# Expert stage of a hybrid encoder: 96 token slots per expert sweep instead of 128

## The reference

```
def moe_swiglu(x, w_router, w_gate, w_up, w_down):
    """Top-2-of-8 SwiGLU experts, softmax over the selected logits (Mixtral)."""
    b, s, d = x.shape
    xt = x.reshape(b * s, d)
    logits = (xt @ w_router).astype(jnp.float32)
    top_val, top_idx = lax.top_k(logits, TOP_K)
    top_w = jax.nn.softmax(top_val, axis=-1)
    gates = jnp.sum(jax.nn.one_hot(top_idx, N_EXPERTS, dtype=jnp.float32) * top_w[..., None], axis=1)
    gates = gates.astype(x.dtype)
    y = jnp.zeros_like(xt)
    for e in range(N_EXPERTS):
        y = y + gates[:, e:e + 1] * swiglu(xt, w_gate[e], w_up[e], w_down[e])
    return y.reshape(b, s, d)
```

## Time and profile before

| | us |
|---|---|
| median of three runs | 1445.77 |
| lowest and highest run | 1441.11, 1446.24 |
| span of the profiled execution | 1439.2 |
| PE busy | 1415.5 |
| DVE busy | 1133.4 |
| ACT busy | 967.7 |
| POOL busy | 127.0 |

### The profile page before, as it was taken

The page is one execution under the profiler, slowest core; times in us unless marked ns, Lnnn a source line. Parts: engine busy times, 40 slices in busy tenths (PEclk is TensorE's granted clock), DMA queues, the critical chain, the costliest instruction groups (busy, mean ns, idle before and its releaser), DMA issues.

```text
span 1439.2 us, 20918 instructions
## 1 busy us (share of the span) xinstructions
PE 1415.5 (98%) x7689; PEld 1215.3 (84%) x7689; DVE 1133.4 (79%) x896; ACT 967.7 (67%) x885; POOL 127.0 (9%) x101
## 2 busy tenths in 40 slices
PE   9989999999999999999999999999999999999996
PEld 8888999999997888888888888888888888888885
DVE  4764555556665988898898898889899898888886
ACT  6574443446574677777777777777777777777774
POOL 4430000000000410010020001002002001000100
PEclk9999999999999999999999999999999999999999
DMA  9306855555432899999999999999999999999992
GB/s 337 131 1 205 243 187 175 185 194 176 147 115 91 307 386 372 368 383 393 380 365 396 381 355 394 387 346 387 395 384 373 394 368 360 394 375 367 397 396 100
DMA packets 205562, 434.91 MB, mean 302 GB/s; under 512 B 8160, under 2 KB 53344, under 8 KB 205520
## 3 DMA queue, kind: packets, MB, share of 16 engines
q1 hardware_dynamic: 198176, 418.01, 79.7%
q0 software_dynamic: 3904, 14.42, 3.3%
q10 hardware_dynamic: 3440, 1.91, 0.7%
HBM read 426.98 MB, written 7.34 MB: 302 GB/s over the span
## 4 chain that ended last, share of the span: by engine, by line
PE 95%; DVE 2%; ACT 1%; DMA 0%; issue 0%; DVEq 0%; SPq 0%; ACTq 0%
PE banks L1501 29%; PE banks L1503 29%; PE banks L1502 29%; PE banks L1734 2%; PE banks L1955 2%; PE banks L1722 1%; DVE w_lo L928 1%; PE banks L1919 0%; PE banks L1659 0%; DMA xres<-in_x 0%; PE banks L1677 0%; PE banks L1709 0%; PE banks L1593 0%; PE banks L1901 0%; PE banks L1527 0%
## 5 line engine op out<-in xcount | busy, mean ns | idle before, releaser
L928 DVE TENSOR_TENSOR w_lo<-raw,w_hi 128x2048 fp32r<-128x2048 f32 (+1 forms) x396 | 906.5, 2301 | 208.8 <-ACT w_hi L497 206.3
L497 ACT CAST w_hi<-raw 128x2048 fp32r<-128x2048 f32 (+1 forms) x396 | 756.4, 1911 | 217.6 <-PE banks L1503 210.2
L1501 PE MATMUL banks<-w_hi,t_hi 128*128 128x512 f32 (+2 forms) x1088 | 416.1, 382 | 3.5 <-DVE w_lo L992 1.9
L1503 PE MATMUL banks<-w_lo,t_hi 128*128 128x512 f32 (+2 forms) x1088 | 411.4, 378 | 0.0
L1502 PE MATMUL banks<-w_hi,t_lo 128*128 128x512 f32 (+2 forms) x1088 | 411.2, 378 | 0.0
L1501 PEld LDWEIGHTS banks<-w_hi,t_hi 128*128 128x128 f32 x1088 | 205.6, 189 | 40.3 <-DVE w_lo L992 2.2
L1503 PEld LDWEIGHTS banks<-w_lo,t_hi 128*128 128x128 f32 x1088 | 205.4, 189 | 37.7
L1502 PEld LDWEIGHTS banks<-w_hi,t_lo 128*128 128x128 f32 x1088 | 205.7, 189 | 36.4 <-issue 0.2
L1501 PE MATMUL banks<-w_hi,h_hi 128*128 128x512 f32 x536 | 209.5, 391 | 0.7 <-DVE w_lo L928 0.7
L1503 PE MATMUL banks<-w_lo,h_hi 128*128 128x512 f32 x536 | 209.2, 390 | 0.0
L1502 PE MATMUL banks<-w_hi,h_lo 128*128 128x512 f32 x536 | 208.7, 389 | 0.0
(11 more groups left out here) (283 smaller groups left out, 955.9 us busy)
## 6 DMA issues: line engine op xcount, KB each, us to landing
raw<-in_moe_w_gate SPq DMA_DIRECT2D x112, 1024.0 KB, 7.8
raw<-in_moe_w_up SPq DMA_DIRECT2D x112, 1024.0 KB, 8.0
raw<-in_moe_w_down SPq DMA_DIRECT2D x112, 1024.0 KB, 7.8
raw<-in_na_w_qkv SPq DMA_DIRECT2D x12, 1024.0 KB, 5.1
raw<-in_ffn_w_gate SPq DMA_DIRECT2D x11, 1024.0 KB, 6.5
raw<-in_ffn_w_up SPq DMA_DIRECT2D x11, 1024.0 KB, 5.4
raw<-in_ffn_w_down SPq DMA_DIRECT2D x11, 1024.0 KB, 4.9
raw<-in_w_in_e SPq DMA_DIRECT2D x6, 1024.0 KB, 18.1
```

The costliest lines, as they stand in the source:

```text
L497: act.copy(w_hi[:, u.part, 0:n], raw[:, u.raw, 0:n]).then_inc(hi_done, 1)
L928: dve.tensor_tensor(w_lo[:, u.part, 0:n], raw[:, u.raw, 0:n], w_hi[:, u.part, 0:n].bitcast(F32), ALU.subtract).then_inc(lo_done, 1)
L1501: pe.matmul(out, a_hi, b_hi, start=start, stop=False)
L1503: return pe.matmul(out, a_hi, b_lo, start=False, stop=stop)
```

## The change

The slots of an expert become 96. The sweep's stationary operands are 96 columns wide, the tiles whose rows are slots use 96 partitions, the turned tiles have 4 x 96 columns instead of 4 x 128, and the indirect transfers move 96 rows. The overflow branch is taken when an expert has more than 96 tokens, and then runs two more sweeps, for places 96 to 191 and 192 to 287. There is one more DRAM tensor for sums, and the constant table is 32 columns wider. The weight loads, their splitting and the number of matmuls in a sweep stay as they are.

```
+SLOTS = 96
+SWEEPS = -(-SEQ // SLOTS)
...
-            with pe.If(n_over > P):
-                moe_sweep(pe, first, middle, edge, last, 1, ahead)
+            with pe.If(n_over > SLOTS):
+                for again in range(1, SWEEPS):
+                    moe_sweep(pe, first, middle, edge, last, again, ahead)
...
# gate_up
-                        last = three(banks[:, bank + i // 2, :], t_hi[:, kk, 0:P], t_lo[:, kk, 0:P],
+                        last = three(banks[0:SLOTS, bank + i // 2, :], t_hi[:, kk, 0:SLOTS], t_lo[:, kk, 0:SLOTS],
                                      hi_w[:, k, :], lo_w[:, k, :], kk == 0, kk == KD - 1)
...
# moe_down
-                    rows(u, range(4), lambda k, t: h_hi[:, slot, (2 * i + k) * P:(2 * i + k + 1) * P],
+                    rows(u, range(4), lambda k, t: h_hi[:, slot, (2 * i + k) * SLOTS:(2 * i + k + 1) * SLOTS],
...
# turn_hid
-                    last = pe.transpose(banks[:, 6, k * P:(k + 1) * P], hid[:, k * P:(k + 1) * P], ident)
+                    last = pe.transpose(banks[:, 6, k * SLOTS:(k + 1) * SLOTS], hid[0:SLOTS, k * P:(k + 1) * P],
+                                        ident[0:SLOTS, 0:SLOTS])
...
# turn_rows
-                    last = pe.transpose(banks[:, 2 + k // 4, (k % 4) * P:(k % 4 + 1) * P],
-                                        x_tok[:, k * P:(k + 1) * P], ident)
+                    last = pe.transpose(banks[:, 2 + k // 4, (k % 4) * SLOTS:(k % 4 + 1) * SLOTS],
+                                        x_tok[0:SLOTS, k * P:(k + 1) * P], ident[0:SLOTS, 0:SLOTS])
...
# ScalarE, VectorE
-                act.copy(h_hi[:, slot, :], banks[:, 6, :]).then_inc(h_hi_done, 1)
+                act.copy(h_hi[:, slot, 0:4 * SLOTS], banks[:, 6, 0:4 * SLOTS]).then_inc(h_hi_done, 1)
...
-                dve.tensor_tensor(h_lo[:, slot, :], banks[:, 6, :], h_hi[:, slot, :].bitcast(F32),
-                                  ALU.subtract).then_inc(h_lo_done, 1)
+                dve.tensor_tensor(h_lo[:, slot, 0:4 * SLOTS], banks[:, 6, 0:4 * SLOTS],
+                                  h_hi[:, slot, 0:4 * SLOTS].bitcast(F32), ALU.subtract).then_inc(h_lo_done, 1)
...
# GpSimd
-                pool.indirect_dma_start(out=x_tok[:], out_offset=None, in_=rows_d,
-                                        in_offset=bass.IndirectOffsetOnAxis(ap=row_i[:], axis=0)).then_inc(x_tok_in, 16)
+                pool.indirect_dma_start(out=x_tok[0:SLOTS], out_offset=None, in_=rows_d,
+                                        in_offset=bass.IndirectOffsetOnAxis(ap=row_i[0:SLOTS], axis=0)).then_inc(x_tok_in, 16)
```

More of the change, by code:

```diff
@@ L288, in trunk @@
         x_tok = part_of(5120, 1024)
-        pick_x = part_of(6144, 256).rearrange("p (t s) -> p t s", t=T)
+        pick_x = part_of(6144, T * SLOTS).rearrange("p (t s) -> p t s", t=T)
         row_i = sb("row_i", [P, 1], U32)
-        sum_d = [nc.dram_tensor(f"moe_sum{i}", (SEQ + P, D), F32, kind="Internal").ap() for i in range(2)]
+        sum_d = [nc.dram_tensor(f"moe_sum{i}", (SEQ + P, D), F32, kind="Internal").ap() for i in range(SWEEPS)]
         y_tok = part_of(6400, 1024)
@@ L475, in _ @@
             n_over = sp.value_load(over[0:1, 0:1], min_val=0, max_val=SEQ)
-            with sp.If(n_over > P):
-                moe_sweep(sp, first, middle, edge, last, 1)
+            with sp.If(n_over > SLOTS):
+                for again in range(1, SWEEPS):
+                    moe_sweep(sp, first, middle, edge, last, again)
             with sp.Else():
@@ L905, in _ @@
             n_over = act.value_load(over[0:1, 0:1], min_val=0, max_val=SEQ)
-            with act.If(n_over > P):
-                moe_sweep(act, first, middle, edge, last, 1)
+            with act.If(n_over > SLOTS):
+                for again in range(1, SWEEPS):
+                    moe_sweep(act, first, middle, edge, last, again)
             with act.Else():
@@ L1487, in _ @@
             n_over = dve.value_load(over[0:1, 0:1], min_val=0, max_val=SEQ)
-            with dve.If(n_over > P):
-                moe_sweep(dve, first, middle, edge, last, 1, ahead)
-                dve.wait_ge(y_add, 2 * 4 + 1)
+            with dve.If(n_over > SLOTS):
+                for again in range(1, SWEEPS):
+                    moe_sweep(dve, first, middle, edge, last, again, ahead)
+                dve.wait_ge(y_add, 4 * SWEEPS + 1)
             with dve.Else():
@@ L1548, in columns, with rows @@
                 return last
-            def rows(u, bank, lhs_hi, lhs_lo, n_t, start, stop):
+            def rows(u, bank, lhs_hi, lhs_lo, n_t, start, stop, n_out=P):
                 pe.wait_ge(lo_done, u.count())
@@ L1558, in rows @@
                             cols = slice(c * HALF, (c + 1) * HALF)
-                            last = three(banks[:, bank[2 * t + c], :], lhs_hi(i, t), lhs_lo(i, t),
+                            last = three(banks[0:n_out, bank[2 * t + c], :], lhs_hi(i, t), lhs_lo(i, t),
                                          hi_w[:, i, cols], lo_w[:, i, cols], start and i == 0, stop and i == 1)
@@ L1910, in slots @@
                 for t in range(T):
-                    last = pe.matmul(banks[:, 7, SEQ:SEQ + 4], pick_x[:, t, :], token_in[:, t, :],
+                    last = pe.matmul(banks[0:SLOTS, 7, SEQ:SEQ + 4], pick_x[:, t, :], token_in[:, t, :],
                                      start=(t == 0), stop=(t == T - 1))
@@ L1947, in moe_down @@
                     u = unit_of(base, *units[i])
-                    rows(u, range(4), lambda k, t: h_hi[:, slot, (2 * i + k) * P:(2 * i + k + 1) * P],
-                         lambda k, t: h_lo[:, slot, (2 * i + k) * P:(2 * i + k + 1) * P], 1, start and i == 0,
-                         stop and i == 1).then_inc(used, 1)
+                    rows(u, range(4), lambda k, t: h_hi[:, slot, (2 * i + k) * SLOTS:(2 * i + k + 1) * SLOTS],
+                         lambda k, t: h_lo[:, slot, (2 * i + k) * SLOTS:(2 * i + k + 1) * SLOTS], 1, start and i == 0,
+                         stop and i == 1, SLOTS).then_inc(used, 1)
             def turn_hid(s):
@@ L1963, in turn_pick @@
                 for t in range(T):
-                    last = pe.transpose(banks[:, 7, t * P:(t + 1) * P], pick_c[:, t, :], ident)
+                    last = pe.transpose(banks[0:SLOTS, 7, t * P:(t + 1) * P], pick_c[:, t, :], ident)
                 last.then_inc(comb_mm, 1)
@@ L2119, in add_rows @@
                 pool.wait_ge(y_free, 2 * n + 2)
-                pool.indirect_dma_start(out=sum_d[sweep], out_offset=bass.IndirectOffsetOnAxis(ap=row_s[:], axis=0),
-                                        in_=y_tok[:], in_offset=None, compute_op=ALU.add).then_inc(sum_in, 16)
+                pool.indirect_dma_start(out=sum_d[sweep], out_offset=bass.IndirectOffsetOnAxis(ap=row_s[0:SLOTS], axis=0),
+                                        in_=y_tok[0:SLOTS], in_offset=None, compute_op=ALU.add).then_inc(sum_in, 16)
                 pool.wait_ge(sum_in, 16 * n + 16)
@@ L2133, in experts @@
                     pool.tensor_copy(place_e.unsqueeze(2), place[:, :, 0:1]).then_inc(pick_step, 1)
[L2134 removed]
+                    pool.wait_ge(pick_step, 2 * sweep)
                     for t in range(T):
@@ L2167, in _ @@
             n_over = pool.value_load(over[0:1, 0:1], min_val=0, max_val=SEQ)
-            with pool.If(n_over > P):
-                experts(1)
+            with pool.If(n_over > SLOTS):
+                for again in range(1, SWEEPS):
+                    experts(again)
             with pool.Else():
```

79 lines of the change are left out of this document (40 added, 39 removed).

## The result

| kernel | median us | median of the quicker executions, us | ratio to before, 95% interval |
|---|---|---|---|
| before | 1441.1 to 1444.7 | 1441.1 | |
| changed | 1447.01 | 1447.0 | 1.0032 [1.0018, 1.0045] |

The forecast was 1438.5 us, with 1424 to 1446.5 as range. The change lost some 6 us where a gain of 7 was forecast.

What follows compares the result with a forecast made beforehand. TensorE's own periods were taken to bound the kernel. Savings of 7.0 + 0.1 + 0.25 + 0.1, taken as 7.3 us, from the 1439.2 us span, plus 6.6, gave 1438.5 us; range 1424 to 1446.5.

Steps and rivals of the forecast that it cites:

- The 4032 matmuls at 0.227 us: Expert-stage products: the period stays 0.227 us with 96 stationary columns, so no change; bounds 0.216 and 0.237 us.
- the first rival: Expert products: the weight load shows in the period, so a narrower load saves 11 us more, 1427.4 us; chance 0.31.
- Transposes: `turn_hid` and `turn_rows`: 96 columns stream instead of 128, 0.025 us saved on each of 280, 7.0 us.
- Slot lookup: `slots`, 16 matmuls with 96 stationary columns: 0.1 us saved, 0.8 at best.
- The jump: Skip of the untaken overflow branch: longer code skipped, but one branch on each engine as before; nothing taken for it.
- Base: Whole kernel: span of 1439.2 us, with the three-run median 6.6 us above it for what lies around the span.
- Drain at a change of shape: Rival at the 63 transpose groups: shape switches drain TensorE, 20.5 us cost less the 7.3 gained, 1459 us; chance 0.11.
- ScalarE, VectorE and transfers: Expert stage: casts, differences and transfers stay hidden, except 0.25 us saved in the last step and some 0.1 at first gather.

Runs made afterwards that it cites:

- the series by themselves: Series of 48 matmuls run alone, without the kernel, at several stationary widths; bfloat16 over 512 columns and plain float over 256 stayed at 0.2158 us.

## Why the prediction was wrong

- *The 4032 matmuls at 0.227 us: the step that failed.* The prediction named this as what decides the case, bounded it at 0.216 and 0.237, and took no change "since where the stream is the limit no row shows an effect of the stationary width". The rows it leaned on, of plain float and bfloat16, are of types that show no effect, as the series by themselves confirm. The measured periods are 0.2300 and 0.2309, and the term put at nothing costs 9.9 us: that is what the run with 128-wide products on good starts takes less than the changed kernel, 1437.1 for 1447.0. (The periods of one middle step would give more, 56 x (48 x 2.6 + 24 x 4.4) ns = 12.9; some 1.7 of it come back in the 0.03 us after each group of transposes.) The price has two causes: the width (11 us alone, in the run with only the products narrow), and the starts of the `h_hi` and `h_lo` slices in 384-byte steps, which cost even slices of 128 columns 3.8 us. They don't add: narrow and badly placed is 0.2309, narrow alone 0.2300.
- *The sign of the first rival.* It let the period fall with the load. The loads of the products fell from 188 to 161 ns (medians, first line of the kernel before, second of the changed one), 27 for 32 columns, which is what the Trainium skill, "TensorE: Matmul & The Clock Gate", section "LDWEIGHTS (loading the stationary operand)", gives for 32 columns; the period rose. The length itself does not agree with the page: 161 ns for 96 columns, where its formula gives 80. A cost above the present one was in the bounds (40 us at most), but had no chance of its own among the cases.

```profile
L1501 PEld LDWEIGHTS banks<-w_hi,h_hi x536: 186/188/192, 160.6 to 1424.7; 128*128 128x128 f32 x179
L1508 PEld LDWEIGHTS banks<-w_hi,h_hi x536: 159/161/192, 160.9 to 1428.1; 128*96 128x96 f32 x149, 128*128 128x128 f32 x30
```

- *Transposes, right in mechanism, a little too high in size.* 82 ns apart for 109, by the count of moving columns; with 88 columns they follow to 75. But a group of four in `turn_hid` saves 0.08 us and not 4 x 0.025, as its way back to the products does not shrink. With the products back at their old speed, the change as a whole gained 6.2 us (1434.9 for 1441.1), where 7.3 were forecast.
- *Slot lookup, too low.* 0.1 was taken and 0.8 was the bound; each lookup takes 0.08 us less of the chain (first the kernel before, then the changed one), some 0.6 in eight of them.

```profile
620.64 0.34 PE banks L1911 x4
```

```profile
621.37 0.26 PE banks L1918 x4
```

- *The jump, wrong.* "I take nothing for it" cost 2.3 us on the path (2.56 for 0.29). The prediction looked at the branch as one instruction and not at how much code lies behind it.
- *Base.* The 6.6 us around the span were 2 for this execution. At the clock of the profiled execution the same sum would have read 1434, and the miss is 13 us and not 8.5. That the measured time lies only 0.5 us above the range is luck.
- *Drain at a change of shape, rightly given little.* The 0.56 us around the four transposes of 96 rows between products of 96 columns, and the 0.59 between products of 128, are less than the 0.67 of before.
- *ScalarE, VectorE and transfers, right.* None was in the path inside the stage; in the last step the two splits took 0.48 and 0.56 us for 0.59 and 0.69.

The sum, from the kernel before to the changed one: -6.2 for what the forecast did count, +9.9 for the products, +2.2 for the jump (1437.1 for 1434.9), together the 5.9 us that were lost. From profile to profile the loss is 5.7 us: 0.4 up to the stage, 3.3 from its first group of transposes to its last (929.4 for 926.1), and 2.0 behind them, of which the jump has 2.3.

Open: why rounded-float matmuls over 512 columns have this period. Off 226.7 ns the periods vary in patterns that mostly repeat after three to seven matmuls, no order in the width fits them, and one width gave two values in two runs. What the load and the stream contend for is not shown.

## What to carry to other kernels

A tile that covers fewer useful rows is not cheaper on TensorE as such: here no rounded-float products over 512 columns ran quicker than those with 128 stationary columns starting on multiples of 256 bytes, and leaving the extra columns as idle filler was worth 9.9 us against cutting them, while transposes follow the columns that stream and may be cut. Before a shape that no row of the same type shows is taken at its old price, run it by itself for 48 instructions. And count the code that a branch skips: put a long jump where its engine waits anyway.

## What the runs showed that I had not expected

- A rounded-float matmul over 512 columns starts every 226.7 ns with well placed slices of 128 stationary columns, and every 229 to 236 ns with 120, 112, 96, 80, 64, 48, 32, 16 or 1 (8 had 226.7 in one run and 231.3 in the other); over 256 columns it is the other way round, 120 against 113 to 118.
- The start of the stationary slice counts: steps of 256 or 512 bytes 226.7 ns, steps of 384 or 64 bytes 233.4, a shift by 128 bytes 232.6, at the same width of 128.
- Jumping over the code of two sweeps instead of one took VectorE 2.3 and ScalarE 2 us longer (2.56 for 0.29, 2.23 for 0.18), though the branch was not taken in either.
